# Attention phase of a hybrid decoder step: the sampled tokens' sums in four steps, a tile's keys and values loaded ahead of its queries

## The chip, the cores and the metric

The kernel is one program on one core of a Trainium2 chip. The metric is the device time of one execution in microseconds (us). The engines run their own instruction streams side by side and wait for each other through semaphores: PE (TensorE, matrix products and transposes; PEld is its weight load), DVE (VectorE), ACT (ScalarE), POOL (GpSimd) and SP (SyncE), which here only issues DMAs and waits.

## What is computed

One inference step over 2048 prompt tokens and 8 sampled tokens: a gated short convolution layer, then keys and values for three dilation groups, then a layer of dilated sliding-window attention whose three group outputs are mixed by their softmax denominators, gated and projected. The change touches only the second layer's attention. For the prompt and for the samples that is, cut down:

```python
# prompt, for each group (window, dilation) = (128,1), (512,4), (2048,16)
s = jnp.einsum('brnqkgd,brnjkd->brnkgqj', qs, ks) * SCALE      # masked to the window
p = jnp.exp(s - logsumexp(s))
o = jnp.einsum('brnkgqj,brnjkd->brnqkgd', p, vs)
# samples, for each group: 8 tokens, 2 key heads, 4 query heads per key head, 128 cached rows and the new one
s = jnp.einsum('btkgd,btnkd->btkgn', qg, kg) * SCALE
p = jnp.exp(s - lse[..., None])
o = jnp.einsum('btkgn,btnkd->btkgd', p, vg)
```

All is in 32-bit floats. The large products are made from operands split into a high and a low part, as three products (high by high, high by low, low by high).

## The kernel before, in words

The convolution layer and the projections come first, to about 1830 us of the profile. The attention phase fills the rest, to the end at 2686 us, and it alone is touched.

**Tiles and chunks.** The attention runs over 48 tiles `a` of 128 queries: 16 of the group with dilation 16, then 16 of the one with dilation 4, then 16 of the one with dilation 1. A tile is cut into chunks `c`, 152 in all, each one bank of scores: two chunks per tile in the first 16 tiles (chunks 0 to 31), two or four in the next 16 (chunks 32 to 87), four in the last 16. Every engine goes through the same loop over `c` with its own share of the work.

**What PE does in a chunk**, in this order: it transposes the probabilities of chunk c+1 (L1832, so a row of that line opens a chunk); makes the scores of c+3 (L1823 to L1825); at a tile's last chunk, transposes the keys of the tile three further on (L1801, it waits for the load of `kv_raw`); makes some steps of the product for the gate (L1875 to L1877; four steps of three products per chunk in chunks 0 to 31, two in chunks 32 to 87); makes one *sample step*, if the chunk has one; makes the values' products (L1851, L1853), for which it needs the high and low probabilities and, at the first chunk of a head, the sums of the chunk before added up by DVE (`add_sums`, L2232).

**Sample steps.** The 8 sampled tokens are worked on group by group in between, one small step per chunk: `queries` (L1888), `keys0`, `keys1` (L1893, transposes of cached keys), `scores0` (L1901, 8 products with 4 columns), `keys2`, `keys3`, `scores1`, `score` (L1905), one chunk without a step while ACT makes the exponentials, `prob` (L1908), `sums` (L1913: 16 products of a 128 x 128 block of cached values with 4 columns of probabilities) and `sum` (L1918). `BEGIN` says at which chunks the three groups begin: 4, 19, 34. DVE copies every step's result out in the same chunk; the copy of the queries into order (L2343, `sample_queries_of`) stands one chunk ahead of the first step and waits for the load of `s_qt_raw`.

**What SP issues.** Also chunk by chunk, in one row: stores of the tiles' parts and of the gate, loads for the gate's rows (L1670) and weights (L1644, it waits until DVE has made the low part of the weights before, `weights_lo`, L2185 or L2188), at chunks BEGIN-4 to BEGIN-1 the four quarters of the samples' cache (L1688), with the second of them also the samples' queries and new rows (L1692, L1693), and at a tile's last chunk `load_tile(a + 4)`: queries (L1648), then keys and values (L1652). An instruction that waits on SP holds up all behind it.

**Transposes' banks.** All transposes and sample steps take turns on two PSUM banks in the order of the list `TURNS`; a turn waits until the turn before the last has been copied out.

Of the kernel before, what the change touches and what calls it, by code (L numbers as in the profile page):

```python
# [27 lines left out]
NS = 8  # L28
# [763 lines left out]
KVH = 2  # L792
# [560 lines left out]
def attention_programs(nc, ctx, q_tiles, kv_rows, partials, ht_tiles, silu_rows, h_rows, o_sample,  # L1353
# [86 lines left out]

        return ("gate", "output")[n // (2 * KT)], n // KT % 2, n % KT

    STEPS = ("queries", "keys0", "keys1", "scores0", "keys2", "keys3", "scores1", "score", "prob", "sums", "sum")
    BEGIN = (4, 19, 34)
    sample_in = {BEGIN[x] + m + (m >= 8): (x, step) for x in range(GROUPS) for m, step in enumerate(STEPS)}
    sample_queries = {BEGIN[x] - 1: x for x in range(GROUPS)}
    sample_exp = {BEGIN[x] + 8: x for x in range(GROUPS)}
    sample_load = {BEGIN[x] - 4 + y: (x, y) for x in range(GROUPS) for y in range(4)}
    SAMPLE_END = BEGIN[-1] + len(STEPS) + 1

    def gated_turns(c):
# [195 lines left out]
    def load_queries(sp, a):  # L1647
        sp.dma_start(q_raw[a % 2][:].rearrange("p (h n) -> p h n", h=HEADS), q_tiles[group(a)][a % NT])\  # L1648
          .then_inc(s_qraw[a % 2], 16)
# [22 lines left out]
    def loads_and_stores(sp):  # L1672
        def load_tile(a):
            if a >= TILES:
                return
            sp.wait_ge(s_qlo, a - 1)
            load_queries(sp, a)
            sp.wait_ge(s_vlo, a - 1)
            sp.wait_ge(s_turned, turned("keys", a - 2))
            load_keys(sp, a)  # L1680

        def load_sample(x, y):

            g = ORDER[x]
            if x > 0:
                sp.wait_ge(s_turned, turned("sample", x - 1, "sums"))
            cached = caches[g].rearrange("b (k d) c -> k d b c", d=DILATIONS[g])[:, 0, :, :]
            sp.dma_start(cache[y][:], cached[:, 2 * y:2 * y + 2, :]).then_inc(s_cache[y], 16)  # L1688
            if y == 1:
                if x > 0:  # L1690
                    sp.wait_ge(s_lo, turned("sample", x - 1, "sum"))
                sp.dma_start(s_qt_raw[:], q_sample[g]).then_inc(s_squeries, 16)  # L1692
                sp.dma_start(s_new[:], new_rows[g].rearrange("r (j d) -> r j d", j=2)).then_inc(s_snew, 16)  # L1693

        def store_gate(z):
            (t, half), n = z_tile(z), z_height(z)
            sp.wait_ge(s_zout, z + 1)
            sp.dma_start(silu_rows[t * P:t * P + n, half * BANK:(half + 1) * BANK], gate_out[z % 2][0:n, :])\
              .then_inc(s_zstore[z % 2], 16)

        def store_part(a):
            sp.wait_ge(s_part, 2 * a + 2)
            sp.dma_start(partials[group(a)][rows(a), :], part(a)).then_inc(s_partstore[a % RING], 16)

        def load_groups(t):

            b = t % 2
            if t < 2:
                for x in range(RING):
                    sp.wait_ge(s_partstore[x], 16 * LAST // RING)  # L1710
            else:
                sp.wait_ge(s_merge, 3 * (t - 2) + 3)
            for g in (1, 2):
                sp.dma_start(parts[b][:, g, :], partials[g][t * P:(t + 1) * P, :]).then_inc(s_g[b], 16)

        def load_gate(j):

            t, n, b = OUT_TILES[j], out_height(j), j % 2
            if j >= 2:
                sp.wait_ge(s_gated, j - 1)  # L1720
            z = Z_JOBS - 1 if t == NT else NT + 1 + t
            for x in range(2):
                sp.wait_ge(s_zstore[x], 16 * len(range(x, z + 1, 2)))
            sp.dma_start(silu_z[b][0:n, :], silu_rows[t * P:t * P + n, :]).then_inc(s_silu[b], 16)

        def load_h(j):

            t, n, b = OUT_TILES[j], out_height(j), j % 2
            if j >= 2:
                sp.wait_ge(s_ystore[b], 16 * (j // 2))  # L1730
            sp.dma_start(h_buf[b][0:n, :], h_rows[t * P:t * P + n, :]).then_inc(s_h[b], 16)

        def store_y(j):
            t, n, b = OUT_TILES[j], out_height(j), j % 2
            sp.wait_ge(s_y, j + 1)
            dst = y_sample if t == NT else y_prompt[t * P:(t + 1) * P, :]
            sp.dma_start(dst, h_buf[b][0:n, :]).then_inc(s_ystore[b], 16)

        load_weights(sp, range(KT, KT + RAW))
        store_gate(0)  # L1740
        store_gate(1)
        load_tile(2)
        load_rows(sp, Z_FIRST + 1)
        store_gate(2)
        load_tile(3)
        for b in range(2):
            sp.wait_ge(s_qstore[b], q_stored)
        for c in range(NCH):
            a, i = place(c)
            if i == 0:  # L1750
                if 1 <= a <= LAST:
                    store_part(a - 1)
                if a >= LAST + 4:
                    store_y(a - LAST - 4)
                    load_h(a - LAST - 2)
            if i == 1 and a >= LAST:
                load_gate(a - LAST)
            if (a, i) == (LAST, 2):
                load_groups(0)
                load_groups(1)  # L1760
                load_h(0)
                load_h(1)
            if c - 1 in gate_end and gate_end[c - 1] + 2 < Z_JOBS:
                load_rows(sp, gate_end[c - 1] + 2)
            if c - 2 in gate_end:
                store_gate(gate_end[c - 2])
            for n in split_in.get(c, ()):
                if n + RAW < SLICES:
                    load_weights(sp, [n + RAW])
            if c in sample_load:  # L1770
                load_sample(*sample_load[c])
            if c == SAMPLE_END + 3:
                sp.wait_ge(s_step, 10)
                sp.dma_start(o_sample.rearrange("b (x d) -> (b x) d", d=HD), s_sums[:, 0, :]).then_inc(s_sout, 16)
                sp.dma_start(post_gain[:], norm_post.partition_broadcast(P)).then_inc(s_gain, 16)
            if c == last_chunk[a]:
                load_tile(a + 4)
            t = merged_in(a)
            if i == 3 and t is not None and t + 2 < NT:
                load_groups(t + 2)  # L1780
        sp.wait_ge(s_gated, NT - 1)
        sp.wait_ge(s_sout, 16)
        sp.dma_start(parts[0][0:NS, 1, 0:D], o_sample).then_inc(s_g[0], 16)
        load_gate(OUT_JOBS - 1)
        for j in range(NT - 4, OUT_JOBS):
            store_y(j)
            if j + 2 < OUT_JOBS:
                load_h(j + 2)
        for b in range(2):
            sp.wait_ge(s_ystore[b], 16 * len(range(b, OUT_JOBS, 2)))  # L1790

    def products(pe):
# [88 lines left out]
        def sample_step(x, step):  # L1881
# [14 lines left out]
            elif step[:6] == "scores":  # L1896
                half = int(step[6:])
                pe.wait_ge(s_lo, turned("sample", x, f"keys{2 * half + 1}"))
                for y in range(8):
                    row = (8 * half + y) * QPK  # L1900
                    last = nc.tensor.matmul(out[:, row:row + QPK], keys_t[y // 4][:, y % 4, :], s_qt[:, row:row + QPK],  # L1901
                                            start=True, stop=True)
            elif step == "score":
                pe.wait_ge(s_lo, turned("sample", x, "scores1"))
                last = nc.tensor.transpose(out[0:SAMPLES, 0:P], s_score_t[:], ident[:])  # L1905
            elif step == "prob":
                pe.wait_ge(s_sexp, x + 1)
                last = nc.tensor.transpose(out[:, 0:SAMPLES], s_score[:, 0:KEYS], ident[0:SAMPLES, 0:SAMPLES])  # L1908
            elif step == "sums":
                pe.wait_ge(s_lo, turned("sample", x, "prob"))  # L1910
                for y in range(NS * KVH):
                    seq, n = y // KVH, y % KVH
                    last = nc.tensor.matmul(out[:, y * QPK:(y + 1) * QPK],  # L1913
                                            cache[seq // 2][:, seq % 2, KVW + n * HD:KVW + (n + 1) * HD],
                                            s_prob_t[:, y * QPK:(y + 1) * QPK], start=True, stop=True)
            else:
                pe.wait_ge(s_lo, turned("sample", x, "sums"))
                last = nc.tensor.transpose(out[0:SAMPLES, 0:P], s_sum_t[:], ident[:])  # L1918
            last.then_inc(s_turned, 1)

# [269 lines left out]
    def sums_and_lows(dve):  # L2190
# [155 lines left out]
        def sample_evacuated(x, step):  # L2346
# [20 lines left out]
                nc.vector.tensor_reduce(s_stat[:, 0, x:x + 1], s_score[:], AX_X, ALU.min).then_inc(s_sleast, 1)  # L2367
            elif step == "prob":
                nc.vector.tensor_copy(s_prob_t[:], src[:, 0:SAMPLES]).then_inc(s_lo, 1)
            elif step == "sums":  # L2370
                nc.vector.tensor_copy(s_sum_t[:], src[:, 0:SAMPLES]).then_inc(s_lo, 1)
            else:
                dve.wait_ge(s_sexp, x + 1)
                nc.vector.scalar_tensor_tensor(out=s_sums[:, x, :], in0=s_new[:, 1, :],
# [266 lines left out]
```

## Time and profile before

| | us |
|---|---|
| three timed runs: median (lowest, highest) | 2687.9 (2674.45, 2691.96) |
| the profiled execution, its own time | 2688.0 |
| its span, from the first to the last instruction | 2686.1 |
| PE busy in the span | 2583.3 |
| PE idle in the attention phase while it waits for `kv_raw` | 12.4, in 7 waits |
| mean granted clock of TensorE over the span | 0.981 |

A granted clock of 1.00 is 2.4 GHz, one of 0.50 is 1.2 GHz; a stretch with a number in between had both. A matmul's busy time overlaps the next one's, so a PE that is shown busy all the time may still be slow. That is why the granted clock of a stretch has to be read beside its busy time.

### The profile page before, as it was taken

How to read it: one execution, taken by the hardware profiler on the slowest of the kernel's cores; microseconds unless marked ns; L12 is line 12 of the kernel's file. 1: busy time of each engine (PE TensorE's matmuls, PEld its weight loads, DVE VectorE, ACT ScalarE, POOL GpSimd, SP SyncE). 2: the span in 40 equal slices, each digit the busy share in tenths (PEclk: the TensorE clock that was granted, in tenths of full speed). 3: DMA queues.
4: the chain of work that ended last, by engine and by line, in shares of the span. 5: the costliest groups of instructions: out<-in, count | busy, mean ns of one | idle time of the engine just before them, and what ended most of it. 6: DMA issues, size and time to landing. Idle time of an engine off the chain costs nothing.

```text
span 2686.1 us, 38106 instructions
## 1 busy us (share of the span) xinstructions
PE 2583.3 (96%) x14140; PEld 2365.6 (88%) x14140; DVE 1161.4 (43%) x2469; ACT 848.4 (32%) x2090; POOL 545.0 (20%) x573
## 2 busy tenths in 40 slices
PE   6999999999999969999999999999999999899997
PEld 5999999999988748778999999998888899788885
DVE  7311112111244333211345454334645665777774
ACT  6211111111145533101000000013545566766662
POOL 1011111111002211111222222223211122233333
PEclk9999999999999989999999999999989899999998
DMA  5222332333365544693354546456665565544441
GB/s 158 92 86 92 101 104 87 95 101 104 101 214 173 177 153 149 191 258 119 87 127 106 131 102 134 104 140 222 230 228 190 176 211 186 184 139 154 166 143 64
DMA packets 302771, 387.96 MB, mean 144 GB/s; under 512 B 78349, under 2 KB 227493, under 8 KB 301114
## 3 DMA queue, kind: packets, MB, share of 16 engines
q1 hardware_dynamic: 297498, 342.41, 42.0%
q10 hardware_dynamic: 5152, 44.01, 5.1%
q8 instruction: 68, 1.11, 0.2%
q14 instruction: 53, 0.43, 0.0%
HBM read 266.69 MB, written 163.68 MB: 160 GB/s over the span
## 4 chain that ended last, share of the span: by engine, by line
PE 44%; DMA 2%; DVE 1%; ACT 1%; issue 1%; SPq 1%; POOL 0%; POOLq 0%; DVEq 0%; ACTq 0%
PE p_pair L1148 6%; PE p_pair L1149 6%; PE p_pair L1150 6%; PE p_pair L1851 3%; PE p_tps L1832 2%; PE p_pair L1936 2%; PE p_pair L1938 2%; PE p_pair L1937 2%; PE p_pair L1875 2%; PE p_pair L1876 2%; PE p_pair L1877 2%; DMA g_kv_raw<-scratch_kv_rows 2%; PE g_score L1825 1%; PE g_score L1824 1%; PE g_score L1823 1%; PE p_pair L1853 1%
## 5 line engine op out<-in xcount | busy, mean ns | idle before, releaser
L281 PE MATMUL a_pair<-a_ht_hi,a_w_hi 128*128 128x412 f32 (+1 forms) x1280 | 448.8, 351 | 2.0 <-DVE a_ht_lo L450 2.0
L282 PE MATMUL a_pair<-a_ht_lo,a_w_hi 128*128 128x412 f32 (+1 forms) x1280 | 447.9, 350 | 0.0
L283 PE MATMUL a_pair<-a_ht_hi,a_w_lo 128*128 128x412 f32 (+1 forms) x1280 | 447.9, 350 | 0.0
L1148 PE MATMUL p_pair<-p_ht_hi,p_q_hi 128*128 128x416 f32 (+1 forms) x960 | 336.1, 350 | 0.5 <-DVE p_turned L1282 0.5
L1149 PE MATMUL p_pair<-p_ht_lo,p_q_hi 128*128 128x416 f32 (+1 forms) x960 | 335.7, 350 | 0.0
L1150 PE MATMUL p_pair<-p_ht_hi,p_q_lo 128*128 128x416 f32 (+1 forms) x960 | 334.4, 348 | 0.0
L281 PEld LDWEIGHTS a_pair<-a_ht_hi,a_w_hi 128*128 128x128 f32 x1280 | 241.5, 189 | 3.0 <-DVE a_ht_lo L450 2.4
L282 PEld LDWEIGHTS a_pair<-a_ht_lo,a_w_hi 128*128 128x128 f32 x1280 | 241.3, 189 | 1.0
L283 PEld LDWEIGHTS a_pair<-a_ht_hi,a_w_lo 128*128 128x128 f32 x1280 | 241.2, 188 | 0.6
L1341 POOL TENSOR_TENSOR p_q_out<-p_q_out,p_turned 128x416 f32<-128x416 f32 (+1 forms) x120 | 142.1, 1200 | 397.7 <-DVE p_turned L1282 326.3
L1280 DVE TENSOR_TENSOR p_q_out<-p_pair,p_table 128x416 f32<-128x416 f32 (+1 forms) x120 | 93.1, 776 | 284.3 <-PE p_pair L1150 150.1
L240 POOL TENSOR_TENSOR a_w_lo<-a_w_raw,a_w_hi 128x1024 fp32r<-128x1024 f32 x32 | 76.2, 2403 | 619.2 <-ACT a_w_hi L341 619.2
L2485 POOL TENSOR_TENSOR g_qt_lo<-g_q_raw,g_qt_hi 128x1024 fp32r<-128x1024 f32 x48 | 114.7, 2390 | 355.9 <-ACT g_qt_hi L2015 275.1
L1148 PEld LDWEIGHTS p_pair<-p_ht_hi,p_q_hi 128*128 128x128 f32 x960 | 180.1, 188 | 3.8 <-DVE p_turned L1282 1.8
L1150 PEld LDWEIGHTS p_pair<-p_ht_hi,p_q_lo 128*128 128x128 f32 x960 | 180.6, 188 | 1.7
L1149 PEld LDWEIGHTS p_pair<-p_ht_lo,p_q_hi 128*128 128x128 f32 x960 | 180.2, 188 | 1.2
L1182 ACT ACTIVATE p_q_hi<-p_q_raw,p_gains 128x256 fp32r<-128x256 f32 x96 | 40.4, 497 | 429.5 <-DMA p_q_raw<-b_w_in 429.5
L1851 PE MATMUL p_pair<-g_v,g_pt_hi 128*128 128x256 f32 x608 | 157.0, 335 | 15.7 <-issue 12.5
L1112 PE MATMUL p_pair<-p_w_hi,p_ht_hi 128*128 128x512 f32 (+1 forms) x408 | 163.9, 402 | 5.0 <-DVE p_w_lo L1234 5.0
L1114 PE MATMUL p_pair<-p_w_hi,p_ht_lo 128*128 128x512 f32 (+1 forms) x408 | 161.3, 395 | 0.0
L2041 ACT ACTIVATE g_probs<-g_score,g_parts 128x256 f32<-128x256 f32 (+1 forms) x384 | 160.6, 435 | 2.2 <-DVE g_parts L2209 2.2
L1113 PE MATMUL p_pair<-p_w_lo,p_ht_hi 128*128 128x512 f32 (+1 forms) x408 | 160.9, 394 | 0.0
(219 smaller groups left out, 5171.1 us busy)
## 6 DMA issues: line engine op xcount, KB each, us to landing
out_cache_kv_g_sample<-cache_kv_g ACTq DMA_DIRECT2D x72, 410.0 KB, 3.7
p_table<-rope_columns SPq DMA_DIRECT2D x60, 416.0 KB, 3.2
scratch_q_tiles<-p_q_out SPq DMA_DIRECT2D x48, 512.0 KB, 5.7
g_q_raw<-scratch_q_tiles SPq DMA_DIRECT2D x48, 512.0 KB, 4.0
scratch_partial<-g_parts SPq DMA_DIRECT2D x32, 520.0 KB, 5.6
g_parts<-scratch_partial SPq DMA_DIRECT2D x32, 520.0 KB, 5.7
a_w_raw<-a_w_in SPq DMA_DIRECT2D x32, 512.0 KB, 5.2
g_rows_hi<-scratch_ht_tiles SPq DMA_DIRECT2D x29, 512.0 KB, 5.6
```

What stands on the lines that cost most here:

```text
L281: nc.tensor.matmul(out, hi, ht_hi[:, k, cols], start=(k == 0), stop=False)
L282: nc.tensor.matmul(out, hi, ht_lo[:, k, cols], start=False, stop=False)
L283: last = nc.tensor.matmul(out, lo, ht_hi[:, k, cols], start=False, stop=(k == KT - 1))
L1112: nc.tensor.matmul(out, hi, w_hi[g % 2][:, k, :], start=(k == 0), stop=False)
L1113: nc.tensor.matmul(out, hi, w_lo[g % 2][:, k, :], start=False, stop=False)
L1114: last = nc.tensor.matmul(out, lo, w_hi[g % 2][:, k, :], start=False, stop=(k == KT - 1))
L1148: nc.tensor.matmul(out, hi, ht_hi[:, k, cols], start=(k == 0), stop=False)
L1149: nc.tensor.matmul(out, hi, ht_lo[:, k, cols], start=False, stop=False)
L1150: last = nc.tensor.matmul(out, lo, ht_hi[:, k, cols], start=False, stop=(k == KT - 1))
L1341: last = nc.gpsimd.tensor_tensor(kept, kept, other, op)
L1851: nc.tensor.matmul(sums[:, h, :, :], pt_hi[c % 2][:, at], v[s][:, n, :, :], start=(y == 0), stop=False)
L2041: last = nc.scalar.activation(probs[c % 2][:, y * width:(y + 1) * width], score[c % 2][:, y * width:(y + 1) * width], ACT.Exp, bias=part(a ...
```

## The change

It does four things. (1) The step `sums` with 16 products becomes four steps `sums0` to `sums3` with four products each, one per chunk; each uses one quarter of the cache, and DVE copies its 16 columns out at once. (2) With 14 steps per group instead of 11, the second and third group begin later: `BEGIN` is 4, 22, 40 instead of 4, 19, 34. (3) The second and third group's cache quarters are loaded each one chunk after the step that frees it (first group: chunks 0 to 3, as before); the samples' queries and new rows are loaded by a call of their own, at chunk 3 for the first group (before: chunk 1), and at chunks 20 and 38 for the others. (4) `load_tile` loads keys and values first and queries second, each behind its own waits.

```diff
-    STEPS = ("queries", "keys0", "keys1", "scores0", "keys2", "keys3", "scores1", "score", "prob", "sums", "sum")
-    BEGIN = (4, 19, 34)
+    STEPS = ("queries", "keys0", "keys1", "scores0", "keys2", "keys3", "scores1", "score", "prob",
+             "sums0", "sums1", "sums2", "sums3", "sum")
+    BEGIN = (4, 22, 40)
-    sample_load = {BEGIN[x] - 4 + y: (x, y) for x in range(GROUPS) for y in range(4)}
+    sample_load = {(0, BEGIN[x - 1] + 11)[x > 0] + y: (x, y) for x in range(GROUPS) for y in range(4)}
+    sample_rows = {(3, BEGIN[x - 1] + 16)[x > 0]: x for x in range(GROUPS)}
...
-            sp.wait_ge(s_qlo, a - 1)
-            load_queries(sp, a)
             sp.wait_ge(s_vlo, a - 1)
             sp.wait_ge(s_turned, turned("keys", a - 2))
             load_keys(sp, a)
+            sp.wait_ge(s_qlo, a - 1)
+            load_queries(sp, a)
...
-                sp.wait_ge(s_turned, turned("sample", x - 1, "sums"))
+                sp.wait_ge(s_turned, turned("sample", x - 1, f"sums{y}"))
...
+            if c in sample_rows:
+                load_sample_rows(sample_rows[c])
...
-            elif step == "sums":
+            elif step[:4] == "sums":
                 pe.wait_ge(s_lo, turned("sample", x, "prob"))
-                for y in range(NS * KVH):
+                for y in range(4 * int(step[4:]), 4 * int(step[4:]) + 4):
...
-            elif step == "sums":
-                nc.vector.tensor_copy(s_sum_t[:], src[:, 0:SAMPLES]).then_inc(s_lo, 1)
+            elif step[:4] == "sums":
+                cols = slice(SAMPLES // 4 * int(step[4:]), SAMPLES // 4 * (int(step[4:]) + 1))
+                nc.vector.tensor_copy(s_sum_t[:, cols], src[:, cols]).then_inc(s_lo, 1)
```

Three places of the instruction order show it. The first is PE in chunk 14, from the end of the gate's products (`g_w`, `g_rows`) over the first group's sums (`g_cache` holds the cached rows, `g_sample_prob_t` the probabilities) to the first of the values' products (`g_v`). Before:

```order
L1876 MATMUL p_pair<-g_w_lo_3484,g_rows_hi_3526 128x512
L1877 MATMUL p_pair<-g_w_hi_3481,g_rows_lo_3528 128x512
L1913 MATMUL p_tps<-g_sample_prob_t,g_cache_3496 128x4 x4
L1913 MATMUL p_tps<-g_sample_prob_t,g_cache_3497 128x4 x4
L1913 MATMUL p_tps<-g_sample_prob_t,g_cache_3498 128x4 x4
L1913 MATMUL p_tps<-g_sample_prob_t,g_cache_3499 128x4 x4
L1851 MATMUL p_pair<-g_v_3513,g_pt_hi_3514 128x256
```

The same place in the changed kernel, where lines have moved by five:

```order
L1881 MATMUL p_pair<-g_w_lo_3484,g_rows_hi_3526 128x512
L1882 MATMUL p_pair<-g_w_hi_3481,g_rows_lo_3528 128x512
L1918 MATMUL p_tps<-g_sample_prob_t,g_cache_3496 128x4 x4
L1856 MATMUL p_pair<-g_v_3513,g_pt_hi_3514 128x256
L1858 MATMUL p_pair<-g_v_3513,g_pt_lo_3516 128x128
```

One quarter of the products stays; the other three stand at the same place of chunks 15, 16 and 17.

The second place is SP from chunk 2 to chunk 3: the gate's weight load, cache quarters, the store of a gate tile, the samples' queries and new rows, and the load of tile 5. Before (queries and new rows are issued earlier, at chunk 1):

```order
L1644 DMA g_w_raw<-b_w_in 128x512
L1688 DMA g_cache_3498<-cache_kv_g 128x2x512
L1698 DMA scratch_silu_rows<-g_out_sb 128x512
L1688 DMA g_cache_3499<-cache_kv_g 128x2x512
L1648 DMA g_q_raw_3489<-scratch_q_tiles 128x1024
L1652 DMA g_kv_raw_3506<-scratch_kv_rows 128x512
```

After:

```order
L1646 DMA g_w_raw<-b_w_in 128x512
L1689 DMA g_cache_3498<-cache_kv_g 128x2x512
L1701 DMA scratch_silu_rows<-g_out_sb 128x512
L1689 DMA g_cache_3499<-cache_kv_g 128x2x512
L1695 DMA g_sample_qt_raw<-scratch_q_sample 128x64
L1696 DMA g_sample_new<-scratch_new_rows 64x256
L1654 DMA g_kv_raw_3506<-scratch_kv_rows 128x512
L1650 DMA g_q_raw_3489<-scratch_q_tiles 128x1024
```

The samples' two loads now stand behind the last quarter of the cache, and the tile's two loads have changed places.

The third place is SP in chunk 31, where tile 19 is loaded. Before:

```order
L1698 DMA scratch_silu_rows<-g_out_sb 128x512
L1644 DMA g_w_raw<-b_w_out 128x512
L1688 DMA g_cache_3497<-cache_kv_g 128x2x512
L1692 DMA g_sample_qt_raw<-scratch_q_sample 128x64
L1693 DMA g_sample_new<-scratch_new_rows 64x256
L1648 DMA g_q_raw_3489<-scratch_q_tiles 128x1024
L1652 DMA g_kv_raw_3506<-scratch_kv_rows 128x512
```

After:

```order
L1701 DMA scratch_silu_rows<-g_out_sb 128x512
L1646 DMA g_w_raw<-b_w_out 128x512
L1654 DMA g_kv_raw_3506<-scratch_kv_rows 128x512
L1650 DMA g_q_raw_3489<-scratch_q_tiles 128x1024
L1706 DMA scratch_partial<-g_parts_3501 128x1040
```

Four loads that stood ahead of the keys and values now stand behind them or at later chunks.

## Rows read from the trace of the kernel before

**Rows 1.** Table by stretch: us, busy of PE, PEld, DVE, ACT, POOL, clock, DMA, GB/s.
```profile
1895.00:1945.00 50.00, 48.20 (x327) 43.11 (x326) 31.28 (x53) 27.93 (x94) 11.34 (x8) 1.00 0.67 226
1949.00:1963.00 14.00, 14.00 (x72) 13.13 (x71) 4.61 (x8) 3.92 (x12) 0.69 (x1) 0.63 0.29 103
1983.00:1994.00 11.00, 7.13 (x26) 5.81 (x27) 2.60 (x5) 2.87 (x11) 2.37 (x1) 0.69 0.87 331
2056.00:2069.00 13.00, 13.00 (x62) 11.80 (x63) 4.81 (x7) 3.38 (x12) 1.66 (x2) 0.61 0.72 244
2080.00:2086.00 6.00, 4.10 (x18) 3.52 (x19) 2.33 (x7) 2.76 (x7) 1.05 (x1) 0.72 0.98 385
2125.00:2140.00 15.00, 15.00 (x66) 13.27 (x64) 7.34 (x13) 6.05 (x18) 2.38 (x1) 0.54 0.52 171
2140.00:2147.00 7.00, 7.00 (x48) 6.96 (x48) 0.92 (x2) 0.76 (x2) 0.00 (x0) 0.76 0.01 2
```

**Rows 2.** Chain of waits (start us, us, what): a scores step and a sums step.
```profile
1904.36 1.68 PE p_tps L1901 x16
1949.55 4.33 PE p_tps L1913 x32
```

**Rows 3.** The same view: a gate product at full and at half clock.
```profile
1878.06 0.24 PE p_pair L1877
1988.41 0.43 PE p_pair L1877
```

**Rows 4.** PE's costliest lines of the attention phase; its timeline: transposes of keys.
```profile
L1801 PE MATMUL p_tps<-p_ident,g_kv_raw 128*128 128x128 f32 x92 | 19.5, 296 | 11.6 <-DMA g_kv_raw<-scratch_kv_rows 11.4
1940.46 0.44 PE L1801 MATMUL p_tps<-p_ident,g_kv_raw 128*128 128x128 f32 x2 [1.25 <-DMA g_kv_raw<-scratch_kv_rows]
1986.87 0.47 PE L1801 MATMUL p_tps<-p_ident,g_kv_raw 128*128 128x128 f32 x1 [4.09 <-DMA g_kv_raw<-scratch_kv_rows]
2081.90 0.48 PE L1801 MATMUL p_tps<-p_ident,g_kv_raw 128*128 128x128 f32 x1 [3.00 <-DMA g_kv_raw<-scratch_kv_rows]
```

**Rows 5.** Chunks 17 and 31: SP's timeline, two landings (cache, queries), chain of waits.
```profile
1978.12 0.43 SPq L1688 DMA_DIRECT2D g_cache<-cache_kv_g  x1
1978.60 0.47 SPq L1648 DMA_DIRECT2D g_q_raw<-scratch_q_tiles  x1
DMA to landing us min/median/max: 6.0/6.0/6.0
DMA to landing us min/median/max: 6.9/6.9/6.9
1979.16 7.67 DMA g_kv_raw<-scratch_kv_rows
2073.75 0.33 SPq L1644 DMA_DIRECT2D g_w_raw<-b_w_out  x1
2076.36 5.50 DMA g_kv_raw<-scratch_kv_rows
```

**Rows 6.** Chunk 3: DVE's, SP's and PE's timelines; landings of that cache quarter, of `s_qt_raw`.
```profile
1880.32 0.23 DVE L2343 COPY g_sample_qt<-g_sample_qt_raw 128x64 f32<-128x64 f32 x1
1880.79 0.44 SPq L1688 DMA_DIRECT2D g_cache<-cache_kv_g  x1
1885.72 0.37 PE L1851 MATMUL p_pair<-g_v,g_pt_hi 128*128 128x256 f32 x1
DMA to landing us min/median/max: 4.6/4.6/4.6
DMA to landing us min/median/max: 3.7/6.5/7.9
```

**Rows 7.** Timelines at chunks 41 and 42: DVE's and PE's.
```profile
2120.15 2.48 DVE L2188 TENSOR_TENSOR g_w_lo<-g_w_raw,g_w_hi 128x512 fp32r<-128x512 f32 x1 [0.63 <-ACT g_w_hi L2008]
2123.60 0.67 DVE L2232 TENSOR_TENSOR g_parts<-p_pair,g_low_sums 128x512 f32<-128x512 f32 x1
2124.38 0.36 PE L1851 MATMUL p_pair<-g_v,g_pt_hi 128*128 128x256 f32 x1 [2.13 <-issue]
```

More of the change, by code:

```diff
@@ L1680, in load_tile, with load_sample_rows @@
             load_keys(sp, a)
+            sp.wait_ge(s_qlo, a - 1)
+            load_queries(sp, a)
         def load_sample(x, y):
-            g = ORDER[x]
             if x > 0:
-                sp.wait_ge(s_turned, turned("sample", x - 1, "sums"))
-            cached = caches[g].rearrange("b (k d) c -> k d b c", d=DILATIONS[g])[:, 0, :, :]
+                sp.wait_ge(s_turned, turned("sample", x - 1, f"sums{y}"))
+            cached = caches[ORDER[x]].rearrange("b (k d) c -> k d b c", d=DILATIONS[ORDER[x]])[:, 0, :, :]
             sp.dma_start(cache[y][:], cached[:, 2 * y:2 * y + 2, :]).then_inc(s_cache[y], 16)
[L1689 to L1693, printed above, removed]
+        def load_sample_rows(x):
+            if x > 0:
+                sp.wait_ge(s_lo, turned("sample", x - 1, "sum"))
+            sp.dma_start(s_qt_raw[:], q_sample[ORDER[x]]).then_inc(s_squeries, 16)
+            sp.dma_start(s_new[:], new_rows[ORDER[x]].rearrange("r (j d) -> r j d", j=2)).then_inc(s_snew, 16)
         def store_gate(z):
@@ L1916, in sample_step @@
             else:
-                pe.wait_ge(s_lo, turned("sample", x, "sums"))
+                pe.wait_ge(s_lo, turned("sample", x, "sums3"))
                 last = nc.tensor.transpose(out[0:SAMPLES, 0:P], s_sum_t[:], ident[:])
```

## The prediction

> **What bounds the kernel now.** I first read where PE idles and at what clock it runs, since PE is busy 2583.3 of 2686.1 us, then who releases it, and then, at each such place, what stood ahead of the releaser on SP or DVE. The profiled execution took 2688.0 us, its span is 2686.1, and the median of the three runs is 2687.9: the sum below is made against 2688.0, and no shift to the median is needed. The lowest run, 2674.45, says that the kernel has spells that don't come in every execution.
>
> The table by stretch [rows 1] shows six places in chunks 14 to 44 where the granted clock is between its two levels, 2.4 and 1.2 GHz, while the first row of the group, 50 us of the same work, stays at 1.00. What is lost is (1 - clock) times the length: 14 x 0.37 = 5.2 us, 11 x 0.31 = 3.4, 13 x 0.39 = 5.1, 6 x 0.28 = 1.7, 15 x 0.46 = 6.9 and 7 x 0.24 = 1.7. Three of the six (5.2, 5.1, 1.7) begin at the sampled tokens' sums, in the three groups. One such step holds PE for 4.3 us with 4-column products, and PE is not idle then: 14.00 of 14 us are busy. A scores step, half as many small products in 1.68 us, stands at 1904 [rows 2], inside the 50 us whose clock stays at 1.00 [rows 1]. The reader is to see that it is the long run of tiny products and not a wait that goes before these three falls. The other three begin just after PE stood still: 4.09 us and 3.00 us for a load of keys and values [rows 4], and 2.13 us at chunk 42 [rows 7]. A wait of 1.25 us at 1940 [rows 4], inside the 50 us at clock 1.00, brings no fall.
>
> Keys and values: PE waits for them 11.4 us after the start of the phase, in six places; without the two long ones the other four share 4.3 us [rows 4].
>
> **The change, part by part.**
>
> *Sums in four.* The same 48 products are made, four per chunk. A part takes a quarter of 4.3 us, 1.1 us, less than the scores step that brings no fall [rows 2], and a full chunk of wide products follows. I take all three falls away: 12.0 us by the clock. At half clock the same gate product takes 0.43 instead of 0.24 us [rows 3], so a microsecond at half clock loses 0.44 and not 0.5; 12.0 becomes 10.6. Bounds: 0, if four tiny products in four chunks running still bring the fall, and 12.0. The products themselves cost what they cost before. DVE gets three more copies per group, nine in all, each bounded by the small copy of 0.23 us [rows 6]; DVE is busy 31.28 of 50 us in the first stretch [rows 1], and PE's need of the copy is a chunk off, so they cost nothing. Without that cover they would cost 2 us.
>
> *Keys and values first.* Ahead of the load stood the queries, 512 KB. At chunk 17 the cache quarter lands 6.0 us after 1978.1, so at 1984.1, the queries 6.9 after 1978.6, at 1985.5, and keys and values 7.67 after 1979.16, at 1986.8 [rows 5]. Taking the queries from in front saves at least the 0.5 us of their issue and at most that and the 1.4 us between the first two landings; I take 1.9. Of the four short waits, 1.1 each on the mean, three keep about 0.2 each: 3.7 of 4.3 us gone. At chunk 17 the cache quarter stays in front, so 4.09 becomes 2.2; but PE now has the last part of the sums (1.1) between this point and the transposes, so 1.1 is left and 3.0 gone. At chunk 31 cache, samples' queries and new rows go from in front too: the load is issued right behind the weights' load, at 2073.75 + 0.33 = 2074.1 instead of 2076.36, 2.2 us earlier, and lands sooner by the queries' share [rows 5]: 3.00 gone. Sum 9.7; with only the issue saved it would be 0.5 in each short place, 1.6 and 2.7: 6.3. The queries land later by what they gave up, up to 1.9 us; ACT takes them two or more chunks after issue, and PE later still. The wait of SP for POOL's low queries now stands behind the keys' load and holds up the same stores as before.
>
> *The two clock falls behind these waits.* With 1.1 us left at chunk 17 and nothing at chunk 31, both under the 1.25 that brings no fall: 3.4 + 1.7 us by the clock, less 0.4 during which PE idled anyway, times 0.88: 4.1.
>
> *Chunk 42.* There PE waits for DVE's sum, 2.13 us: DVE had a weights' low part of 2.48 us at chunk 41 and behind it the samples' `score` copies, and only then the add that PE waits for [rows 7]. With the third group later, chunk 41 has `keys0` and chunk 42 `keys1` in place of `score` and nothing: PE comes about 0.7 us later, DVE about 0.4 earlier, so about 1.0 is left. Chunk 37 has a similar low part, covered today by a scores step (1.68 us) that moves to chunk 43; I book 1.0 us of new wait for it. Time won by waits: 0.1. But 1.0 is under 1.25, so the fall goes: 6.9 x 0.88 = 6.1. Bounds: 0 and 6.1.
>
> *The samples' queries at chunk 3.* This is the cost. Today the copy runs at 1880.32 without a wait, since its data were loaded two chunks before. Now SP issues them behind the gate's store and the last cache quarter, at 1880.79 + 0.48 = 1881.3, just when DVE reaches the copy, and DVE waits for the whole landing. Three landings took 3.7, 6.5 and 7.9 us; the cache quarter in front lands 4.6 after 1880.79, at 1885.4 [rows 6]. I take 1885.6, just behind it, since it is small (32 KB). Behind the copy stand the add that PE needs for chunk 4's values (0.67 as at chunk 42 [rows 7]), the low probabilities, the next minima. Copy and add end at 1886.5; PE comes to the values at 1885.7 [rows 6]: about 1.0 us of PE, no fall. Bounds: 3.7 gives an end at 1885.9, a cost of 0.2; 7.9 gives 1890.1, 4.4 us, and a fall of up to 5. For the other groups the copy stands one chunk after the load and PE's use another chunk later; I take nothing, at most 1 us.
>
> Sum: 10.6 + 9.7 + 4.1 + 0.1 + 6.1 - 1.0 = 29.6 us. 2688.0 - 29.6 = 2658.4, said as **2658**.
>
> **The rivals.**
>
> *Half the clock falls come back* (2666). A residual wait at chunk 17, 37 or 42 of 1.5 to 2 us lies between the 1.25 that brings no fall and the 2.13 that does, and PE, faster before it, comes earlier to meet DVE, which is no faster. Losing the 6.1 and 2 us of wait: 2688.0 - 21.5 = 2666.5.
>
> *The falls at the sums stay* (2669). For it speaks that four parts in chunks running are still the same products, and that something else could sit at all three places; against it, that the scores step brings no fall [rows 2]. Then 10.6 is not won: 2669.0. The Trainium skill (TensorE: Matmul & The Clock Gate, HAM oscillation) names idle gaps between groups of matmuls, such as a wait for a DMA, as what brings the clock down. By that page the sums, in which PE does not idle, would not be the cause and splitting them would win nothing; the trace disagrees, with PE busy 14.00 of 14 us before and in the first fall [rows 1].
>
> *The load order saves little* (2664). SP reaches `load_tile` only when DVE lets it, and if transfers share the queue rather than follow each other, only the issue time is saved: 6.3 for 9.7, and the wait at chunk 17 stays near 2.5, so its fall (3.4 less 0.4, times 0.88: 2.6) stays too. 6.0 less: 2664.4. With the fall behind chunk 31 as well it would be 2666.
>
> *Slower: DVE's wait for the samples' queries* (2690 and more). Place: chunks 3, 21, 39. If each landing were so late that PE waits w and falls to half clock for 10 us, each costs w + 4.5. The three take up the 29.6 won and the 1.0 booked from w = 5.7 us on, a landing about 9.2 us after issue at chunk 3. The latest of the three landings took 7.9 us, and the second and third group have a chunk more, so this is hardly likely.
>
> **Chances.** As forecast, 2650 to 2662: 0.50. Falls that come back at the waits: 0.20. Load order that saves less: 0.12. Falls at the sums stay: 0.08. Better than forecast, since the copy at chunk 3 costs nothing and chunk 37 no wait, to 2647: 0.06. Slower: 0.04. About 1%, 27 us, is what a measurement of this kernel tells from no change: 2661 is the mark. Most of the first case (0.47) and the better one (0.06) lie below, with 0.03 of the others: faster 0.56, same 0.40, slower 0.04. The range from 2648 to 2674 leaves out the slower case, the best edge and those where two rivals meet.
>
> **What would show it.** The four parts of the sums at about 1 us each, and the clock at 1.00 from chunk 5 to the end of the group with dilation 4. Waits of L1801's successor for `kv_raw` of about 1.5 us in sum after the start, the longest at chunk 17's load. A wait of DVE for `s_qt_raw` of about 5 us at chunk 3 with about 1 us on PE. If the clock falls right after a part of the sums, the first term is wrong; if it falls after a wait at chunk 17, 37 or 42, the fourth or fifth is; if keys still come late by 2 us, the second is.

## The result, and the profile after

| | before | changed |
|---|---|---|
| median of 8 runs (lowest, highest), us | 2681.1 (2674.5, 2692.0) | 2661.6 (2656.1, 2664.9) |
| the profiled execution's own time | 2688.0 | 2659.8 |
| its span | 2686.1 | 2658.0 |
| mean granted clock over the span | 0.981 | 0.988 |

The ratio is 0.9924, with an interval of 0.9905 to 0.9942: 0.76% faster, about 20 us. A second measurement, beside the last experiments, gave 0.9919 (0.9905 to 0.9934). The two profiled executions lie 28.2 us apart, more than the medians do. The experiments explain that: the kernel before differs from one execution to the next by more than the changed one (17.5 us against 8.8 between the highest and the lowest of the 8 runs).

Where the 28.2 us went is seen in the table by stretch, over the attention phase of both kernels. The columns are those of [rows 1]: length, busy time of PE, PEld, DVE, ACT and POOL (instructions in brackets), granted clock, share and rate of the DMAs. Before:

```profile
1835.00:2686.10 851.10, 801.04 (x5068) 704.63 (x5066) 547.56 (x1234) 485.86 (x1470) 235.48 (x319) 0.95 0.52 177
```

After:

```profile
1834.00:2658.00 824.00, 779.97 (x5067) 686.19 (x5066) 549.84 (x1243) 485.31 (x1470) 235.47 (x318) 0.98 0.54 183
```

The phase is 27.1 us shorter. PE idles 44.0 us in it instead of 50.1, which is 6.0 us; the other 21.1 us are busy time: the same products at a higher clock. The trace's records of the granted clock say the same. From the phase's first chunk to the end of the group with dilation 4 they hold 58.0 us at half clock before and 10.2 after; the difference of 47.8 us, at the 0.44 us that a microsecond at half clock loses by [rows 3], is 21.0.

The stretches after that answer to [rows 1]: the 50 us of the first row; the first group's four parts of the sums; the wait for the load issued at chunk 17; the second group's parts; the wait behind chunk 37; the begin of the third group; chunks 42 to 44; the third group's parts. A load issued at chunk 17 is needed by PE at chunk 19, one of chunk 31 at chunk 33; "at chunk 17" and "at chunk 31" name the load, here as in the prediction.

```profile
1892.00:1942.00 50.00, 50.00 (x346) 45.13 (x345) 32.82 (x56) 30.10 (x102) 12.47 (x8) 1.00 0.69 231
1945.00:1969.00 24.00, 24.00 (x175) 22.20 (x174) 14.42 (x25) 14.08 (x48) 5.46 (x3) 1.00 0.64 231
1969.00:1981.00 12.00, 11.02 (x75) 9.84 (x74) 6.70 (x12) 6.71 (x23) 3.12 (x2) 1.00 0.97 338
2054.00:2070.00 16.00, 16.00 (x121) 14.90 (x120) 9.97 (x25) 8.19 (x22) 3.12 (x2) 1.00 0.67 229
2078.00:2084.00 6.00, 4.81 (x33) 4.08 (x32) 5.04 (x9) 3.38 (x12) 2.65 (x2) 1.00 0.65 206
2088.00:2098.00 10.00, 7.97 (x48) 7.30 (x48) 5.33 (x16) 4.11 (x11) 1.04 (x1) 0.83 0.37 144
2100.00:2115.00 15.00, 14.43 (x109) 13.48 (x110) 12.13 (x21) 7.48 (x24) 2.85 (x2) 1.00 0.64 195
2134.00:2151.00 17.00, 17.00 (x128) 15.93 (x127) 8.39 (x28) 8.62 (x26) 3.12 (x2) 1.00 0.56 200
```

All three places of the sums stand at 1.00; one stretch of this table is below 1.00, at 2088, where the third sample group begins. PE's waits between the phase's first transposes and the last group (engine, tile, line, who was waited for; us in total, times, longest):

```profile
PE p_tps L1893 <- DVE g_sample_qt L2348: 1.8, 1, 1.8
PE p_tps L1837 <- ACT g_probs L2046: 1.8, 1, 1.8
PE p_pair L1880 <- DMA g_rows_lo<-scratch_ht_tiles: 1.7, 1, 1.7
PE p_tps L1806 <- DMA g_kv_raw<-scratch_kv_rows: 1.3, 2, 1.0
PE p_pair L1856 <- POOL g_v L2496: 1.2, 1, 1.2
PE p_pair L1856 <- DVE g_parts L2237: 1.1, 3, 0.6
PE p_tps L1898 <- DVE g_sample_keys_t L2358: 0.7, 1, 0.7
```

Keys and values cost 1.3 us instead of the 11.4 of [rows 4]. The first and the third line are new (the second, at the opening, was there before). The next view shows where the first comes from: the copy of the samples' queries on DVE at chunk 3, the add behind it for which PE waits in chunk 4, the issue of the third group's queries on SP, and its copy and PE's first step.

```profile
1882.70 0.23 DVE L2348 COPY g_sample_qt<-g_sample_qt_raw 128x64 f32<-128x64 f32 x1 [4.97 <-DMA g_sample_qt_raw<-scratch_q_sample]
...
1883.62 0.36 PE L1856 MATMUL p_pair<-g_v,g_pt_hi 128*128 128x256 f32 x1 [0.28 <-DVE g_parts L2237]
...
2082.19 0.43 SPq L1695 DMA_DIRECT2D g_sample_qt_raw<-scratch_q_sample  x1
...
2089.63 0.22 DVE L2348 COPY g_sample_qt<-g_sample_qt_raw 128x64 f32<-128x64 f32 x1 [4.21 <-DMA g_sample_qt_raw<-scratch_q_sample]
2089.99 0.27 PE L1893 MATMUL p_tps<-p_ident,g_sample_qt 128*64 128x128 f32 x1 [1.80 <-DVE g_sample_qt L2348]
```

At chunk 3 DVE waits 4.97 us and PE pays 0.28. At chunk 39 DVE waits 4.21 us, PE pays 1.80 in the chunk behind it, and 3.41 us at half clock begin at 2091.0.

### The profile page after: what moved, and what is told of

It reads as the page before. It is cut to its first block and busy times, and to the rows that moved or that the text cites. A ratio compares the mean times of both kernels' runs of the same rounds, so it can differ in the third digit from the quotient of the medians.

```text
span 2658.0 us, 38124 instructions
## 1 busy us (share of the span) xinstructions
PE 2564.4 (96%) x14140; PEld 2348.9 (88%) x14140; DVE 1166.1 (44%) x2478; ACT 847.6 (32%) x2090; POOL 543.2 (20%) x573
```

## The experiments

Medians of experiments stand beside a before that was run again on the same chip (57 runs on three chips in all, median 2685.3, from 2673.8 to 2693.6). "Half-clock stretches" are read from the trace's records of the granted clock.

**One part at a time.** First the load order alone:

```diff
 # the kernel before
-            sp.wait_ge(s_qlo, a - 1)
-            load_queries(sp, a)
             sp.wait_ge(s_vlo, a - 1)
             sp.wait_ge(s_turned, turned("keys", a - 2))
             load_keys(sp, a)
+            sp.wait_ge(s_qlo, a - 1)
+            load_queries(sp, a)
```

> The kernel before with only the load order changed: a tile's keys and values ahead of its queries. My theory: PE's waits for keys and values after the start fall from 11.4 to about 2 us and the two half-clock stretches behind the waits of 4.09 and 3.00 us go (4.1), the three stretches that begin at the sums and the one behind chunk 42 stay: about 13 us less than before, 2668 beside a before of 2681. Rival, only the issue time of the queries is saved: 6 us less, 2675, with waits of about 2.5 us left at chunk 17 and 31 and a fall behind each.

Measured: 2676.0, ratio 0.9970 (0.9956 to 0.9984), so about 8 us. The waits went as my theory said, the time did not:

```profile
PE p_tps L1801 <- DMA g_kv_raw<-scratch_kv_rows: 3.2, 3, 1.6
```

Keys and values cost 3.2 us, and neither of the two longest waits left, 1.58 and 1.30 us, has a half-clock stretch behind it. Half clock stands behind two of the three sums (6.83 us each), behind chunk 42 (6.83) and behind a new wait of 1.31 us for the samples' queries (3.41). Much of what was missing against 13 us seems to lie in the base: in the execution of the last experiment, before waits 9.1 us for keys and values, not 11.4, and has 1.5 us of falls behind these waits, not 4.1.

Then all but the load order:

```diff
 # the changed kernel
+            sp.wait_ge(s_qlo, a - 1)
+            load_queries(sp, a)
             sp.wait_ge(s_vlo, a - 1)
             sp.wait_ge(s_turned, turned("keys", a - 2))
             load_keys(sp, a)
-            sp.wait_ge(s_qlo, a - 1)
-            load_queries(sp, a)
```

> The changed kernel with the load order of before (queries first): the sums in four steps, the groups' later begins and the moved loads of the samples. My theory: no half-clock stretch begins at the sums (10.6 us) nor at chunk 42 (6.1), while waits for keys and values of some 8 to 11 us stay: about 16 us less than before, 2665. Rival, the falls at the sums have another cause and stay: 2676, with stretches of about 10 us at half clock at two or three of the sums' chunks.

Measured: 2668.4, ratio 0.9947 (0.9929 to 0.9965), about 14 us. Waits for keys and values come to 6.3 us. No half-clock stretch begins at the sums or at chunk 42; four short ones of 3.41 us each follow waits of 1.50 to 1.84 us.

Then only the later begins, with the sums in one step:

```diff
 # the kernel before
-    BEGIN = (4, 19, 34)
+    BEGIN = (4, 22, 40)
```

> The kernel before with only the begins of the second and third group moved to chunks 22 and 40; the sums stay one step of 16 products, the loads keep their distance to the begins. My theory: the long run of tiny products takes its half-clock stretch of about 10 us with it to chunks 32 and 50, the one behind chunk 42 goes: 6 us less than before, 2675. Rival, the falls belong to what else stands in chunks 30 and 44 and don't follow: 13 us less, 2668.

Measured: 2677.2, ratio 0.9970 (0.9957 to 0.9984). The low clock moved with the second and the third group's sums to their new chunks, as the table by stretch shows at the three steps, and the stretch around chunk 42, the last row, is at 1.00:

```profile
1950.00:1964.00 14.00, 14.00 (x82) 13.02 (x81) 5.01 (x9) 4.30 (x13) 1.40 (x2) 0.76 0.31 109
2068.00:2080.00 12.00, 12.00 (x72) 11.57 (x71) 4.14 (x14) 4.45 (x12) 0.77 (x2) 0.72 0.45 166
2149.00:2161.00 12.00, 12.00 (x72) 11.37 (x71) 3.22 (x12) 2.94 (x9) 0.91 (x1) 0.72 0.18 72
2107.00:2122.00 15.00, 14.31 (x107) 12.94 (x107) 12.40 (x22) 8.59 (x22) 5.52 (x3) 1.00 0.78 277
```

So the fall belongs to the sums and not to their old places. Shares by these ratios: load order 8 us, begins 8, and the sums in four (with the moved loads of the samples) on top of the begins 0.9970 - 0.9947 = 0.23%, 6 us. They add up to 22, near the 20 to 22 of the whole change; each is uncertain by 4 us or more, so the sum proves little. The last two kernels ran side by side, and there the medians lie 8.8 us apart.

**The run of tiny products put back.** The fourth part makes its four products four times over.

```diff
 # the changed kernel, step "sums3" alone
-                for y in range(4 * int(step[4:]), 4 * int(step[4:]) + 4):
+                part = range(4 * int(step[4:]), 4 * int(step[4:]) + 4)
+                for y in [y for _ in range(4 if step == "sums3" else 1) for y in part]:
```

> The changed kernel whose fourth sums step makes its four products four times over (16 tiny products in a row again, the results the same); all else as in the changed kernel. Added work is 12 products of about 0.27 us in three groups, 9.7 us. My theory, the run of tiny products lowers the clock: a half-clock stretch begins at chunk 17, 35 and 53, about 3.5 us each, so 9.7 + 10.6 more than the changed kernel, 2682. Rival, the falls before came from something else: 9.7 more, 2671, and the clock stays at 1.00 there.

Measured: 2676.5, ratio 0.9971 (0.9956 to 0.9985). The clock falls at all three fourth parts:

```profile
1968.00:1982.00 14.00, 14.00 (x83) 12.71 (x82) 6.50 (x9) 4.85 (x14) 3.09 (x2) 0.76 0.68 237
2076.00:2088.00 12.00, 12.00 (x69) 11.38 (x68) 4.51 (x14) 3.66 (x11) 0.00 (x0) 0.72 0.97 355
2160.00:2170.00 10.00, 10.00 (x66) 9.43 (x64) 4.18 (x14) 2.80 (x10) 0.00 (x0) 0.83 0.48 182
```

This is the plainest evidence for the mechanism: nothing waits, PE is busy 36 of 36 us, the loads and begins are those of the changed kernel. The size was wrong. By the ratios the run costs 0.47 to 0.52%, 13 to 14 us, between my theory's 20 and the rival's 10. The added products take 2.68 us per group at full clock (3.63 us in place of 0.95), 8.0 in all; the half-clock stretches are 6.83, 6.83 and 3.41 us, which at 0.44 cost 7.5. That makes 15.5.

**Two steps of eight, and sixteen dealt out.**

```diff
 # the changed kernel
-             "sums0", "sums1", "sums2", "sums3", "sum")
+             "sums0", "sums1", "sum")
...
-                for y in range(4 * int(step[4:]), 4 * int(step[4:]) + 4):
+                for y in range(8 * int(step[4:]), 8 * int(step[4:]) + 8):
...
```

> The changed kernel with the sums in two steps of eight products. My theory: a step takes about 2.1 us, near the scores step of eight products (1.68 us) that brings no fall, so no half-clock stretch at the sums and the time within 2 us of the changed kernel's 2661.6. Rival, four products were needed and eight are too many: falls of 3.5 us at some of the six steps, 2665 to 2680.

Measured: 2670.0, ratio 0.9939 (0.9920 to 0.9958). A step takes 1.85 us and none of the six brings a fall, as my theory said. The time is not within 2 us of the changed kernel's and lies in the rival's range, though without the rival's falls; the intervals of the two ratios overlap. In its profile two waits, 1.79 us for keys and values at chunk 17 and 1.98 us for the samples' queries, each have 3.41 us at half clock behind them. Whether they belong to the two steps or to the execution, this run doesn't tell, and so the cause of the lost time stays open.

```diff
 # the kernel before
-            for z, k in gate_steps[c]:
+            for y, (z, k) in enumerate(gate_steps[c]):
                 gate_step(z, k)
+                if sample_in.get(c, (0, ""))[1] == "sums":
+                    sums_piece(sample_in[c][0], y, len(gate_steps[c]))
...
```

> The kernel before with the 16 products of the sums dealt out in the same chunk, four behind each of the four steps for the gate (eight behind each of two, where a chunk has two). Same chunk, same products, no change in loads or begins. My theory: no run of more than four or eight tiny products is left, so the falls at the sums go: about 10 us less than before, 2671. Rival, the small products of a chunk lower the clock wherever they stand in it: the falls stay, 2681.

Measured: 2676.2, ratio 0.9965 (0.9951 to 0.9980), 9 us. The first two groups' sums, four products at a time, stand at clock 1.00. In the third group's chunk, with two gate steps, eight products stand behind each, and there 10.24 us at half clock begin at 2121.0, at the end of the first run of eight and 1.1 us before the second begins. So eight in a row can be enough, as the rival of the experiment before had it. The first group's chunk and the third's:

```profile
1945.00:1959.00 14.00, 14.00 (x105) 12.94 (x104) 6.71 (x13) 6.91 (x22) 3.09 (x2) 1.00 0.54 188
...
2119.00:2134.00 15.00, 15.00 (x83) 14.16 (x82) 5.30 (x14) 4.21 (x16) 0.00 (x0) 0.66 0.33 111
```

**What the sums in four bring under the final order.**

```diff
 # the kernel before, with the load order of the changed kernel
-    BEGIN = (4, 19, 34)
+    BEGIN = (4, 22, 40)
```

> The changed kernel itself, beside the two kernels that follow on the same chip. Every theory expects the time it had, 2661.6, within 2 us in the ratio to before.

> The kernel before with the new load order and the later begins together, the sums still one step of 16 products; what it lacks to the changed kernel is the sums in four (and the moved loads of the samples). If the run of 16 costs a stretch of 3.4 to 6.8 us at half clock in each group, as the runs with it show so far, it stands 5 to 9 us above the changed kernel. If the falls at the sums cost the 10.6 us that I forecast, it stands 10 to 12 above it. Rival, the sums in four bring nothing of their own: the same time as the changed kernel.

Measured: 2662.8 for the changed kernel and 2666.8 without the sums in four, ratio 0.9927 (0.9911 to 0.9943). The three falls are there, 6.83, 6.83 and 3.41 us, 7.5 us of loss. But this kernel loads the samples' queries earlier and so lacks the changed kernel's wait at chunk 39 with its fall (2.08 us and 1.5 in the trace of this second execution). 7.5 less 3.6 is 3.9, near the 4.0 between the medians, which is under both of the ranges expected. But the difference of the means, 3.1 us, is uncertain by some 3.5, so the times alone do not exclude the rival; the three falls in the trace speak against it.

**The late queries.**

```diff
 # the changed kernel
-    sample_rows = {(3, BEGIN[x - 1] + 16)[x > 0]: x for x in range(GROUPS)}
+    sample_rows = {(1, BEGIN[x - 1] + 15)[x > 0]: x for x in range(GROUPS)}
```

> The changed kernel with the samples' queries and new rows loaded earlier: chunk 1 for the first group, one chunk earlier for the others. My theory: DVE's three waits for the samples' queries (10.6 us in sum) shrink to under 4, PE's 1.80 us wait at the begin of the third group and the 3.41 us at half clock behind it go: 3 to 4 us less than the changed kernel, 2658 beside its 2661.6. Rival, PE then waits as long at the next of DVE's or the loads' dues there: no change, 2661.

Measured: 2660.6, ratio 0.9920 (0.9904 to 0.9937). DVE's copy for the third group no longer waits, as its timeline shows:

```profile
2087.70 0.22 DVE L2348 COPY g_sample_qt<-g_sample_qt_raw 128x64 f32<-128x64 f32 x1
```

The place has neither PE's wait nor the fall; the table by stretch has it at 1.00:

```profile
2080.00:2100.00 20.00, 18.12 (x125) 15.79 (x124) 15.73 (x33) 12.53 (x36) 6.17 (x4) 1.00 0.62 219
```

The 3 to 4 us can't be seen in the time: the ratio is the changed kernel's own.

**All of SP's loads by need.** With the edit above, also:

```diff
+            if c - 1 in gate_end and gate_end[c - 1] + 2 < Z_JOBS:
+                load_rows(sp, gate_end[c - 1] + 2)
             if i == 0:
                 if 1 <= a <= LAST:
                     store_part(a - 1)
...
-            if c - 1 in gate_end and gate_end[c - 1] + 2 < Z_JOBS:
-                load_rows(sp, gate_end[c - 1] + 2)
...
-            if c in sample_load:
-                load_sample(*sample_load[c])
...
             if c == last_chunk[a]:
                 load_tile(a + 4)
+            if c in sample_load:
+                load_sample(*sample_load[c])
```

> The changed kernel with the samples' rows a chunk earlier, each tile's loads ahead of the cache quarter of the same chunk, and the gate's rows ahead of the store of a tile's part. If PE's waits of 0.98 us at chunk 17, 1.70 us at chunk 32 and 1.80 us at chunk 39 in the changed kernel are due to the order of SP's loads, all three go, with the 3.41 us at half clock behind the last: 5 to 6 us less than the changed kernel. Rival, PE meets the next engine as late: within 2 us of it.

Measured: 2659.3, ratio 0.9901 (0.9884 to 0.9919), 3.5 us below the changed kernel on the same chip. The means differ by 4.3, uncertain by some 3.5 to 4, so it is probably the better kernel. All three waits are gone, and the fall with them. Between the start and the last group no half-clock stretch is left. A new wait took part of the gain. The gate's rows (the list of DMA issues: size, us to landing) and PE's first product with them:

```profile
g_rows_lo<-scratch_ht_tiles SPq DMA_DIRECT2D x1, 512.0 KB, 11.7
```

```profile
1984.95 0.50 PE L1880 MATMUL p_pair<-g_w_hi,g_rows_hi 128*128 128x512 f32 x1 [2.35 <-DMA g_rows_lo<-scratch_ht_tiles]
```

They now stand behind the queries and a cache quarter of the chunk before, and the landing takes 11.7 us.

**The kernel before, once more.**

> The kernel before once more, with a profile. If the half-clock stretches of its first profile are in part a matter of the execution, some of the six between chunks 14 and 44 are shorter or absent here, and its waits for keys and values are below 11.4 us; if they belong to the kernel alone, all six are there at the same lengths.

Measured: this profiled execution took 2671.4 us, below all timed runs of before. Its phase, and the first two groups' sums in one step of 16:

```profile
1834.00:2669.60 835.60, 789.05 (x5066) 694.63 (x5064) 547.23 (x1234) 484.38 (x1469) 232.11 (x315) 0.97 0.53 180
...
1946.00:1960.00 14.00, 14.00 (x105) 13.01 (x104) 6.80 (x12) 6.90 (x24) 2.68 (x2) 1.00 0.50 162
2042.00:2054.00 12.00, 12.00 (x93) 11.21 (x92) 6.89 (x10) 5.72 (x16) 3.10 (x2) 1.00 0.57 192
```

The same step in the same place left the clock at 1.00 twice. From the first chunk to the end of the group with dilation 4 this execution has 30.7 us at half clock where the first profile has 58.0. Its waits for keys and values are 9.1 us where the first has 11.4. In the timed runs clock and time go together: of the 57, six with a mean clock of 0.984 average 2679 us, eleven with 0.979 or less 2690.

## Why the prediction was right, point by point

The changed kernel's profiled execution took 2659.8 and its median is 2661.6, where I said 2658; both are inside the range, and the direction was right. The chance went wrong: I gave 0.56 to a gain of over 1%, and it is 0.76%. That 2658 came so near is in part luck. I forecast 29.6 us of gain, and by the two ratios it is 20 to 22. The sum was made against one execution of before, at 2688.0, which had much low clock, and I said that no shift to the median was needed; the median of the eight runs is 2681.1. Against that one execution the phase did gain 27.1 us.

*Sums in four: mechanism right, size too large.* Over all thirteen traces, 15 of 18 runs of 16 products have a half-clock stretch that begins in the run or within 1.5 us behind it; 0 of 77 runs of four have one, and 0 of 78 scores steps of eight. Of the eight runs of eight sums products one has. By the rule of the Trainium skill that I weighed against it (TensorE: Matmul & The Clock Gate, HAM oscillation), which names idle gaps, the sums would not have been the cause; the runs disagree, with PE busy 36 of 36 us around the three falls of the experiment. But the 18 runs have 95.6 us at half clock among them, 5.3 each, where my 10.6 us stand for 8.0 each. Times 0.44 and three that is 7.0 us.

*Keys and values first: right in the waits.* I forecast that 1.7 us would be left; 1.3 were, 0.98 of them at chunk 17, where I had 1.1, and none at chunk 31. The term of 9.7 holds for the profiled execution (10.1). In the second one there were only 9.1 us of such waits in all.

*The two falls behind them: too large.* I booked 4.1 us. In the second execution the wait of 2.60 us at chunk 17 has no fall and that of 2.84 at chunk 31 one of 3.41 us, worth 1.5. Together with the waits the load order was worth 8 us by its own run, not 13.8.

*Chunk 42: right.* No wait for DVE's sum was left there; 0.71 us remained at the copy of `keys1`, and the fall of 13.65 us is gone. I forecast 1.0 and no fall. The later begins alone brought 8 us by their ratio; my 6.2 lies within its interval (4 to 12). Behind chunk 37 came the new wait that I booked: 1.19 us for 1.0. The profile names POOL's low values, which ended at 2080.95, but DVE's add ended within 0.01 us of them.

*The samples' queries: right at chunk 3, wrong at chunk 39.* I had the landing "just behind" the cache quarter and a wait of about 5 us on DVE: it was 4.97. PE paid 0.28 us, not 1.0: measured against the same place of before, PE came to the values 0.3 us later, and DVE's add ended 0.3 us earlier, than I had it. The step that failed is "for the other groups the copy stands one chunk after the load and PE's use another chunk later; I take nothing, at most 1 us". A chunk there takes about 4 us, and the load lands 7.4 us after its issue, behind tile 21's queries and a store of 520 KB: 1.80 us of PE and 1.5 of clock. So the term that I put at nothing was 3.3 us. The rival that ended slower had this mechanism; where it needed 10.2 us at each of three places, it cost 3.3 at one.

*Not foreseen:* 1.70 us for the gate's rows at chunk 32. Their load lands 9.4 us after issue, behind keys, queries and a store. The profile of before has no wait at this place.

Of the first rival, falls that come back at the waits, none came at the chunks that it names (17, 37, 42), and the six of [rows 1] are gone; one came at chunk 39, so my sign of a clock at 1.00 from chunk 5 on was not met in full. *The falls at the sums stay* fell with the runs that did one part alone. *The load order saves little* fell by its mechanism: alone, the load order left waits of 1.58 and 1.30 us, without the falls that this rival kept. Its price did come, though: 13.8 less its 6.0 is 7.8 us, and 8 were measured.

## What to carry to other kernels

Read the granted clock beside the busy time, chunk by chunk, and price a fall of the clock by its mean over several executions, not by the one that the profile caught. A step of many tiny products is worth dealing out over chunks of wide products even where no engine waits for it. A load that moves nearer to its use must be counted in microseconds of landing behind what is queued ahead of it, not in chunks, since chunks differ in length.

## What the runs showed of the hardware that was not expected

Half clock does not follow from the program alone. A run of 16 tiny products brought 10.24 us at half clock, 6.83, 3.41 or none. Of the waits of PE in the thirteen traces, between the phase's first chunk (the wait at its opening left out) and the last group, none of the 22 between 0.88 and 1.28 us has a fall that begins in it or within 2 us behind it; of 29 between 1.30 and 2.35 us 14 have one, and of six between 2.60 and 4.09 five. Eight of the waits of 0.88 us and more stand ahead of wide gate products, up to 2.35 us long, and none of these has one; of six ahead of the samples' first step, from 1.31 to 2.08 us, five have. What decides it in a single case stays open.
